# A conformer layer on one NeuronCore: x1 in one VectorE instruction from PSUM, three buffers behind silu, the layer norm and the gate in another order, three ada units ahead of x

## The chip, the cores and the metric

The kernel runs on one core of a Trainium2 chip. Its time is device time in microseconds (us); below, the median of three runs. The engines are PE (TensorE matmul; PEld is its weight load), DVE (VectorE), ACT (ScalarE), POOL (GpSimd) and SP (SyncE, which here only issues DMAs). Each engine has its own instruction stream, written by hand, and engines meet only at semaphores, so an instruction that waits holds up all that stands behind it on its engine.

## What is computed

One decoder layer (`DEPTH = 1`, so only mixer kind 0) on 512 tokens with 2048 features: adaLN modulation, RMS norm, conformer convolution, gated residual, RMS norm, squared-ReLU MLP, gated residual, RMS norm.

```python
def rms_norm(x, g):
    return x * lax.rsqrt(jnp.mean(x * x, axis=-1, keepdims=True) + EPS) * g

def conformer_conv(h, w_in, b_in, w_dw, b_dw, ln_g, ln_b, w_out, b_out):
    u = h @ w_in + b_in
    a, gt = jnp.split(u, 2, axis=-1)
    u = a * jax.nn.sigmoid(gt)
    u = causal_depthwise_conv_31(u, w_dw) + b_dw
    u = jax.nn.silu(layer_norm(u, ln_g, ln_b))
    return u @ w_out + b_out

cs = jax.nn.silu(c)
sh1, sc1, g1, sh2, sc2, g2 = split(cs @ ada_w + ada_b, 6)
h = rms_norm(x, norm1_g) * (1 + sc1) + sh1
x = x + g1 * conformer_conv(h, ...)
h = rms_norm(x, norm2_g) * (1 + sc2) + sh2
x = x + g2 * (jnp.square(jax.nn.relu(h @ w1)) @ w2)
return rms_norm(x, final_g)
```

(The three functions are shortened; `causal_depthwise_conv_31` stands for the library call.)

## The kernel before

**Layout.** Activations lie with features on the 128 partitions: 16 chunks of 128 features by 512 tokens. All is float32. A product of fp32 precision is made of three matmuls: each operand is split in a high part (`whi`, `hhi`, `dhi`, rounded to fp32r by ACT) and a low part (`wlo`, `hlo`, `dlo`, the remainder, by DVE or POOL), and PE adds hi*hi, hi*lo and lo*hi.

**Units.** Weights come in units of 128 x 2048 (1 MB). SP loads them into the four slots of `raw`, ACT makes `whi` (L625, `split_hi`), DVE (L942, `split_lo`) or POOL (L1255) makes `wlo`, and PE runs 48 matmuls of 512 columns on them. There are only two slots of `whi` and `wlo`, so the split of a unit waits for the unit two before it. The stages in order of time, named by their first unit:

- **A0**, 8 units: the first half of w_in, "outer": all eight PSUM banks collect at once while the chunks of h come one by one.
- **A1**, 24 units: the other columns of w_in, one bank each ("inner", `inner_unit`). For a feature chunk c the even bank holds the value half and the odd bank the gate half; ACT makes the sigmoid, DVE the product (`glu`, L986), and DVE, ACT and POOL share the 31 taps of the convolution: ACT begins two PSUM sums (`BEGIN`) and makes products (`SIDE`) that POOL adds up (L1283), DVE does the rest (L1002, `conv`). For chunk 15, the last, PE does ten taps with diagonal weights (L518), and DVE fourteen.
- **The layer norm** needs sums over features: PE multiplies by a column of ones (`token_sums`, L462; 128x1 outputs), DVE makes mean and 1/variance (L1034 to L1041), ACT the square root (L634), PE spreads the four columns over all partitions (`spread`, L476, into a PSUM bank), and ACT copies mean and 1/std from PSUM to SBUF (`mu`, `rstd`, L638 and L640).
- **B0**, 8 outer units: the first half of w_out. For each chunk `z(k)` has DVE subtract the mean (L1050), multiply by `rstd` (L1058) and make `hlo` (L931), and ACT make silu (L773) and `hhi` (L777). silu has two buffers, so the silu of chunk k waits for `hlo` of k-2.
- **B1**, 8 inner units: the second half of w_out. x1 = x + g1*(y + b_out): ACT reads a bank and makes g1*y + g1*b_out into `sig` (`gated`, L791), DVE adds x (L1091), ACT squares into `sq` (L798), DVE adds up the squares (L951, one `sq` buffer).
- **C0** and on: the MLP, 8 outer units, then alternating units of w2 and w1, and at the end the last norm, in which DVE makes 11 chunks (L1248) and POOL 5 (L1298), and SP stores them (L386).

**Modulation.** The product with `ada_w` is not done on PE. `ada_reduce(a)` (L925, DVE) multiplies one 128 x 2048 unit by silu(c) and sums it; there are 96 such units, 1 MB each, loaded into four homes (two in `adar`, two slots of `raw`). The tables `ADA_LN`, `ADA_B0`, `ADA_B1`, `ADA_C0` say how many of them DVE does in the layer norm and behind each unit of B0, B1 and C0. Units 0 to 31 (sh1 and sc1) are done in A0, units 32 to 47 hold g1, 48 to 63 sc2, 64 to 79 sh2. Before, `gate1` (L1065, L1068) makes g1 and g1*b_out when all 48 are done.

**keep_busy** (L470) is a run of matmuls of 512 columns whose result nobody reads.

The order on every engine is as the code is written; SP's loads stand in one queue.

## Time and profile before

| | |
|---|---|
| median of 3 runs | 2037.58 us (2036.48 to 2037.75) |
| the profiled execution | 2036.65 us, of it span 2034.8 us |
| PE busy | 1979.2 us (97%) |
| DVE busy | 1074.0 us (53%) |
| ACT busy | 678.8 us (33%) |
| POOL busy | 258.6 us (13%) |
| DMA | 300.73 MB, mean 148 GB/s |
| PE waits for ACT sig L654 / DVE hlo L931 / ACT sig L791 | 11.8 / 8.4 / 4.9 us |
| PE waits for ACT hhi L645 / DVE quad L951 / ACT st L634 | 4.0 / 3.6 / 3.5 us |

The span runs from the first to the last instruction; 1.85 us lie around it in the profiled execution. PE is busy nearly throughout, but busy also counts fillers (`keep_busy`), one-column matmuls and matmuls at the lower of PE's two clock levels, which take twice as long. So the places to look at are those where a stage begins: the start, the layer norm, the step from B0 to B1, that from B1 to C0, and the end. From 640 to 2015 us PE does its matmuls with no gap.

### The profile page before, as it was taken

The numbers are of one execution on the slowest core, as the hardware profiler recorded it, in microseconds if no ns is written. First come the engines' busy times: TensorE is split into PE (matmuls) and PEld (weight loads), VectorE is DVE, ScalarE is ACT, GpSimd is POOL, SyncE is SP. The second block draws the span as 40 slices with busy tenths as digits, with TensorE's granted clock in tenths as the row PEclk, the third lists the DMA queues.
The fourth block names the chain that finished last, engine by engine and source line by source line (L and its number), as shares of the span: only waits on it lengthen the run. The fifth ranks groups of instructions, "written<-read, shape, count | busy, mean of one in ns | idle before, by whom it ended". The sixth has DMA issues, their size and how long they took to land.

```text
span 2034.8 us, 21613 instructions
## 1 busy us (share of the span) xinstructions
PE 1979.2 (97%) x8658; PEld 1619.2 (80%) x8658; DVE 1074.0 (53%) x1159; ACT 678.8 (33%) x747; POOL 258.6 (13%) x145
## 2 busy tenths in 40 slices
PE   6899999999999999999999999999999999999996
PEld 3678888778787888888888888888888888888885
DVE  5989999868897876233223223323322322333244
ACT  5454645543433322321331232123123213212333
POOL 0019999810000000000000000000000000000001
PEclk9999999989999999999999999999999999999998
DMA  9962222247796566222222222222222222222212
GB/s 396 378 268 101 103 88 99 103 166 288 301 402 230 222 247 251 103 104 85 101 100 88 100 103 89 97 103 91 94 103 84 102 103 85 100 103 85 100 62 83
DMA packets 46084, 300.73 MB, mean 148 GB/s; under 512 B 4704, under 2 KB 4704, under 8 KB 10976
## 3 DMA queue, kind: packets, MB, share of 16 engines
q1 hardware_dynamic: 46048, 300.29, 39.6%
q8 instruction: 18, 0.29, 0.1%
q14 instruction: 18, 0.15, 0.0%
HBM read 296.08 MB, written 4.19 MB: 148 GB/s over the span
## 4 chain that ended last, share of the span: by engine, by line
PE 88%; DVE 8%; DMA 1%; ACT 1%; issue 0%; SPq 0%; DVEq 0%; ACTq 0%
PE ps L395 58%; PE ps L400 29%; DVE raw L925 2%; DVE adar L925 2%; DVE wlo L942 1%; DMA adar<-ada 1%; DVE hlo L931 1%; PE ps L484 1%; DVE quad L938 0%; DMA xb<-xT 0%; DVE ps L1002 0%; DVE xb L1248 0%; ACT hhi L777 0%; PE ps L476 0%; ACT whi L625 0%
## 5 line engine op out<-in xcount | busy, mean ns | idle before, releaser
L395 PE MATMUL ps<-hhi,whi 128*128 128x512 f32 (+1 forms) x1792 | 652.1, 391 | 11.8 <-ACT sig L791 4.9
L395 PE MATMUL ps<-hlo,whi 128*128 128x512 f32 (+1 forms) x1792 | 651.8, 390 | 7.3 <-DVE hlo L931 7.3
L625 ACT ACTIVATE whi<-raw 128x2048 fp32r<-128x2048 f32 x176 | 336.3, 1911 | 616.1 <-PE ps L400 615.1
L400 PE MATMUL ps<-hhi,wlo 128*128 128x512 f32 (+1 forms) x1792 | 435.1, 389 | 0.0
L942 DVE TENSOR_TENSOR wlo<-raw,whi 128x2048 fp32r<-128x2048 f32 x151 | 346.0, 2291 | 121.5 <-ACT whi L625 121.5
L395 PEld LDWEIGHTS ps<-hhi,whi 128*128 128x128 f32 x1792 | 336.9, 189 | 87.2 <-issue 9.5
L395 PEld LDWEIGHTS ps<-hlo,whi 128*128 128x128 f32 x1792 | 336.9, 188 | 79.6 <-issue 6.2
L395 PE MATMUL ps<-dhi,whi 128*128 128x512 f32 x1024 | 397.0, 389 | 0.0
L395 PE MATMUL ps<-dlo,whi 128*128 128x512 f32 x1024 | 397.0, 389 | 0.0
L400 PEld LDWEIGHTS ps<-hhi,wlo 128*128 128x128 f32 x1792 | 336.4, 188 | 69.9
L1181 DVE SCALAR_TENSOR_TENSOR xb<-ps,modb,xb 128x512 f32<-128x512 f32 x128 | 90.3, 746 | 363.2 <-PE ps L400 353.6
L400 PE MATMUL ps<-dhi,wlo 128*128 128x512 f32 x1024 | 253.9, 389 | 0.0
L1177 DVE TENSOR_TENSOR dlo<-quad,dhi 128x512 fp32r<-128x512 f32 x56 | 38.8, 693 | 392.3 <-ACT dhi L850 392.3
L1002 DVE SCALAR_TENSOR_TENSOR ps<-xb,pr,ps 128x502 f32<-128x502 f32 (+22 forms) x359 | 231.4, 728 | 3.2 <-ACT ps L702 3.2
L395 PEld LDWEIGHTS ps<-dhi,whi 128*128 128x128 f32 x1024 | 192.3, 188 | 40.0
L400 PEld LDWEIGHTS ps<-dhi,wlo 128*128 128x128 f32 x1024 | 192.2, 188 | 39.9
L395 PEld LDWEIGHTS ps<-dlo,whi 128*128 128x128 f32 x1024 | 192.1, 188 | 39.9
L1298 POOL TENSOR_TENSOR xb<-xb,rstd 128x512 f32<-128x512 f32 x5 | 6.2, 1272 | 1606.8 <-ACT rstd L640 1606.8
L844 ACT ACTIVATE quad<-ps 128x512 f32<-128x512 f32 x56 | 33.5, 598 | 412.8 <-PE ps L400 412.8
L1255 POOL TENSOR_TENSOR wlo<-raw,whi 128x2048 fp32r<-128x2048 f32 x25 | 115.8, 4631 | 147.7 <-ACT whi L625 147.7
L925 DVE SCALAR_TENSOR_TENSOR adar<-adar,csb 128x2048 f32<-128x2048 f32 x40 | 90.8, 2283 | 16.0 <-DMA adar<-ada 15.9
L925 DVE SCALAR_TENSOR_TENSOR raw<-raw,csb 128x2048 f32<-128x2048 f32 x42 | 96.0, 2298 | 3.7 <-DMA raw<-ada 3.7
(122 smaller groups left out, 772.6 us busy)
## 6 DMA issues: line engine op xcount, KB each, us to landing
raw<-w SPq DMA_DIRECT2D x176, 1024.0 KB, 4.8
raw<-ada SPq DMA_DIRECT2D x56, 1024.0 KB, 7.0
adar<-ada SPq DMA_DIRECT2D x40, 1024.0 KB, 7.3
xb<-xT SPq DMA_DIRECT2D x8, 1024.0 KB, 8.7
out<-xb SPq DMA_DIRECT2D x5, 512.0 KB, 4.2
out<-xb SPq DMA_DIRECT2D x6, 256.0 KB, 3.7
csb<-c SPq DMA_DIRECT2D x1, 1024.0 KB, 4.7
quad<-c SPq DMA_DIRECT2D x1, 1024.0 KB, 6.8
```

Source lines behind the costliest of these rows:

```text
L395: return pe.matmul(ps[:, bank, :], whi[:, slot, tile * P:(tile + 1) * P], x, start=first, stop=False, skip_group_check=True)
L400: return pe.matmul(ps[:, bank, :], wlo[:, slot, tile * P:(tile + 1) * P], x, start=False, stop=last, skip_group_check=True)
L484: last = pe.matmul(ps[0:1, 6, :], ones[:], x_squares[k % 2][:], start=k == 0, stop=k == KC - 1, skip_group_check=True)
L625: act.activation(whi[:, q % WS, :], raw_slot(q), ACT.Copy).then_inc(whi_done, 1)
L844: act.activation(relus[j % 2][:], ps[:, bank, :], ACT.Relu).then_inc(relu_done, 1)
L925: dve.scalar_tensor_tensor(s, s, 1.0, cs[:], ALU.mult, ALU.mult, accum_out=mod[:, a:a + 1]).then_inc(ada_used, 1)
L931: dve.tensor_tensor(ch(hlo, k), src[:], f(ch(hhi, k)), ALU.subtract).then_inc(hlo_done, 1)
L942: dve.tensor_tensor(wlo[:, q % WS, :], raw_slot(q), f(whi[:, q % WS, :]), ALU.subtract).then_inc(wlo_done, 1)
L1002: dve.scalar_tensor_tensor(out, ch(xb, c, 0, T - back), col("w_dw", c * TAPS + j), out, ALU.mult, ALU.add).then_inc(dv, 1)
L1177: dve.tensor_tensor(ch(dlo, j % BLK), squares[j % 2][:], f(ch(dhi, j % BLK)), ALU.subtract).then_inc(dlo_done, 1)
L1181: dve.scalar_tensor_tensor(ch(xb, n), ps[:, 4 + n % 4, :], modb[:, M_G2 + n:M_G2 + n + 1], ch(xb, n), ALU.mult, ALU.add).then_inc(x2_done, 1)
L1255: pool.tensor_tensor(wlo[:, q % WS, :], raw[:, q % RAW, :], f(whi[:, q % WS, :]), ALU.subtract).then_inc(wlo_done, 1)
```

## The change

- **Start.** SP loads ada units 0, 1 and 2 ahead of x, and ada unit 3 ahead of the first weight unit. ACT squares x into four buffers; DVE adds two squares each, and PE sums eight pairs in place of 16 squares.
- **1/std.** ACT takes the root straight from the sums in PSUM (scale 1/D, bias eps) and DVE the reciprocal; before, DVE did scale and reciprocal, ACT the root. In the first norm DVE's reciprocal stands behind ACT's root, which stands behind `split_hi(0)`. In the later norms DVE reads 1/std of the first chunk from PSUM and copies it to `rstd` itself.
- **Chunk 15.** Its gate half comes before its value half (the two last units of A1 change places), so that its sigmoid is made during the last unit. DVE has 13 taps for it, POOL five additions in place of four.
- **Layer norm.** Of three ada units one is left, and it stands ahead of the last glu. The 16 fillers ahead of B0 go.
- **B0.** silu has three buffers (`sig` is the third).
- **B1.** g1 is made in two halves. ACT adds g1*b_out to x beforehand (`bias_x`), and DVE makes x1 with one instruction that reads the bank. The first eight x1 follow one another. Squares have two buffers.
- **B1 to C0.** PE sums the last square straight from `sig`; fillers (2, 2 and 4) stand between its steps in place of 8 ahead of C0. DVE's split of unit C0+1 comes behind the first chunks of h2. Of the ada units 1, 14, 20 and 15 are done in the layer norm, B0, B1 and C0; before, 3, 14, 19 and 14.
- **End.** 3 and 4 fillers; DVE's last products wait for the spread alone, and PE spreads a second time for ACT's copy, which POOL uses.

```diff
-SIDE_LAST = 5
+SIDE_LAST = 6
...
-ADA_LN = 3
-ADA_B0, ADA_B1, ADA_C0 = (0, 0, 1, 1, 3, 3, 3, 3), (0, 2, 3, 3, 3, 3, 3, 2), (2, 2, 2, 2, 2, 2, 1, 1)
+ADA_LN = 1
+ADA_B0, ADA_B1, ADA_C0 = (0, 0, 1, 1, 3, 3, 3, 3), (1, 2, 3, 3, 3, 3, 3, 2), (3, 2, 2, 2, 2, 2, 1, 1)
...
-        x_squares = (sig, pacc)
-        scaled, normed, silus = (ta, s1), (tb, s2), (sq, pacc)
+        x_squares = (sig, pacc, tb, sq)
+        scaled, normed, silus = (ta, s1), (tb, s2), (sq, pacc, sig)
         normed2 = (ta, s1, tb, s2)
+        x1_squares = (sq, sig)
...
             load_ada0(0)
-            load_x(0)
-            load_x(1)
             load_ada0(1)
-            load_x(2)
-            load_x(3)
+            load_ada0(2)
+            for i in range(4):
+                load_x(i)
             sp.dma_start(pr[:], par).then_inc(par_in, 16)
-            load_ada0(2)
+            load_ada0(3)
             load_unit0(0)
-            load_ada0(3)
...
-            pe.wait_ge(s2_done, LATE + 1)
             pe.wait_ge(glu_done, KC)
-            token_sums(2, 0, s2, True)
...
-            keep_busy(16, 6, B0 + 1)
+            pe.wait_ge(rstd_done, 3)
             outer_units(B0, KC)
...
             for s in range(2):
-                pe.wait_ge(yg_done, s + 1)
+                pe.wait_ge(x1_done, s + 1)
                 inner_unit(s, s, B1 + s)
...
-            pe.wait_ge(ss1_done, KC)
-            token_sums(2, 0, ssum, True).then_inc(stat_done, 1)
+            pe.wait_ge(ss1_done, KC - 1)
+            token_sums(2, 0, ssum, True)
+            keep_busy(2, 5, C0)
+            pe.wait_ge(x1sq_done, KC)
+            token_sums(2, 0, sig, False).then_inc(stat_done, 1)
+            keep_busy(2, 5, C0)
             pe.wait_ge(root_done, 3)
             spread(3, 8)
-            keep_busy(8, 5, C0 + 1)
+            keep_busy(4, 5, C0 + 1)
...
+            def root(n, bank):
+                act.wait_ge(stat_done, n)
+                if n == 1:
+                    act.wait_ge(eps_set, 1)
+                act.activation(st[:, 4:8], ps[:, bank, 0:4], ACT.Sqrt, scale=1.0 / D, bias=eps[:]).then_inc(var_done, 1)
...
             split_hi(0)
-            root(1, 7)
+            root(1, 5)
+            copy_rstd(1, 7)
...
+            def bias_x(n):
+
+                act.wait_ge(xr_in[n // 4], 16)
+                act.activation(ch(xb, n), ch(xb, n), ACT.Identity, bias=g1b[:, n:n + 1]).then_inc(x1_biased, 1)
...
+            act.wait_ge(small, SMALL_G1 - 2)
+            for n in range(8):
+                bias_x(n)
+            split_hi(B1 + 1)
+            for n in range(8):
+                x1_square(n)
             act.wait_ge(small, SMALL_G1)
...
+            for n in range(8, KC):
+                bias_x(n)
+            for j in range(7):
+                split_hi(B1 + 2 + j)
+                x1_square(8 + j)
...
+            def inverse(n):
+                dve.wait_ge(var_done, n)
+                dve.reciprocal(st[:, 8:12], st[:, 4:8]).then_inc(root_done, 1)
...
-            ada_reduce(2)
-            dve.wait_ge(stat_done, 1)
-            variance(5)
+            inverse(1)
             ada_reduce(3)
             split_lo(0)
...
-                dve.wait_ge(yg_done, n + 1)
-                dve.wait_ge(xr_in[n // 4], 16)
-                dve.tensor_tensor(ch(xb, n), sig[:], ch(xb, n), ALU.add).then_inc(x1_done, 1)
+                if n < 7:
+                    dve.wait_ge(bank_done, 7 + n + 1)
+                else:
+                    dve.wait_ge(unit_done, B1 + n - 7)
+                dve.wait_ge(x1_biased, n + 1)
+                dve.scalar_tensor_tensor(ch(xb, n), ps[:, n if n < 8 else n % 2, :], modb[:, M_G1 + n:M_G1 + n + 1],
+                                         ch(xb, n), ALU.mult, ALU.add).then_inc(x1_done, 1)
```

How the order of instructions moves is shown at three places. The first is DVE from the last tap of chunk 15 to the first chunk of B0; `raw` and `adar` rows of 128x2048 are ada units. Before:

```order
484 L1002 SCALAR_TENSOR_TENSOR ps<-xb,pr,ps 128x492
485 L1009 TENSOR_TENSOR quad<-ps,quad 128x512
486 L1015 TENSOR_TENSOR xb<-ps,quad 128x512
487 L1016 TENSOR_TENSOR xb<-xb,ps 128x491
488 L925 SCALAR_TENSOR_TENSOR raw,mod<-raw,csb 128x2048
489 L1034 TENSOR_SCALAR st<-ps 128x4
490 L925 SCALAR_TENSOR_TENSOR raw,mod<-raw,csb 128x2048
491 L1037 TENSOR_TENSOR st<-st 128x4
492 L1039 SCALAR_TENSOR_TENSOR st<-ps,st 128x4
493 L1040 TENSOR_SCALAR st<-st 128x4
494 L1041 RECIPROCAL st<-st 128x4
495 L925 SCALAR_TENSOR_TENSOR adar,mod<-adar,csb 128x2048
```

The same place in the changed kernel (line numbers are its own):

```order
493 L1022 SCALAR_TENSOR_TENSOR ps<-xb,pr,ps 128x492
494 L1029 TENSOR_TENSOR quad<-ps,quad 128x512
495 L1035 TENSOR_TENSOR xb<-ps,quad 128x512
496 L1036 TENSOR_TENSOR xb<-xb,ps 128x491
497 L1059 TENSOR_SCALAR st<-ps 128x4
498 L1061 TENSOR_TENSOR st<-st 128x4
499 L1063 SCALAR_TENSOR_TENSOR st<-ps,st 128x4
500 L1064 TENSOR_SCALAR st<-st 128x4
501 L1065 RECIPROCAL st<-st 128x4
502 L1073 TENSOR_TENSOR quad<-xb,quad 128x512
503 L1085 TENSOR_TENSOR quad<-quad,ps 128x512
504 L1088 COPY rstd<-ps 128x512
```

Three ada units have left this stretch, and a copy of 1/std has come in behind the first chunk.

The second place is DVE from the last unit split of B0 to the first x1 (L1091, and L1124 in the changed kernel). Before:

```order
558 L942 TENSOR_TENSOR wlo<-raw,whi 128x2048
559 L925 SCALAR_TENSOR_TENSOR adar,mod<-adar,csb 128x2048 x2
560 L1065 TENSOR_TENSOR modb<-mod,pr 128x16
561 L1068 TENSOR_TENSOR g1b<-modb,pr 128x16
562 L925 SCALAR_TENSOR_TENSOR raw,mod<-raw,csb 128x2048
563 L1091 TENSOR_TENSOR xb<-sig,xb 128x512 x3
```

And now:

```order
560 L943 SCALAR_TENSOR_TENSOR adar,mod<-adar,csb 128x2048 x2
561 L1096 TENSOR_TENSOR modb<-mod,pr 128x8
562 L1098 TENSOR_TENSOR g1b<-modb,pr 128x8
563 L943 SCALAR_TENSOR_TENSOR raw,mod<-raw,csb 128x2048
564 L960 TENSOR_TENSOR wlo<-raw,whi 128x2048
565 L943 SCALAR_TENSOR_TENSOR raw,mod<-raw,csb 128x2048
566 L943 SCALAR_TENSOR_TENSOR adar,mod<-adar,csb 128x2048 x2
567 L960 TENSOR_TENSOR wlo<-raw,whi 128x2048
568 L943 SCALAR_TENSOR_TENSOR raw,mod<-raw,csb 128x2048 x2
569 L943 SCALAR_TENSOR_TENSOR adar,mod<-adar,csb 128x2048
570 L1124 SCALAR_TENSOR_TENSOR xb<-ps,modb,xb 128x512 x8
```

The gate (two rows of 128x8) has moved ahead of two splits; three ada units still stand between the last split of B0 and the first x1.

The third place is SP's queue at the start. Before, and then now:

```order
1 L270 DMA csb<-c 128x2048
2 L264 DMA adar<-ada 128x2048
3 L267 DMA xb<-xT 128x4x512 x2
4 L264 DMA adar<-ada 128x2048
5 L267 DMA xb<-xT 128x4x512 x2
6 L277 DMA pr<-par 128x736
7 L264 DMA raw<-ada 128x2048
8 L258 DMA raw<-w 128x2048
9 L264 DMA raw<-ada 128x2048
```

```order
1 L279 DMA csb<-c 128x2048
2 L273 DMA adar<-ada 128x2048 x2
3 L273 DMA raw<-ada 128x2048
4 L276 DMA xb<-xT 128x4x512 x4
5 L285 DMA pr<-par 128x736
6 L273 DMA raw<-ada 128x2048
7 L267 DMA raw<-w 128x2048
```

The first weight unit (`raw<-w`) was the ninth transfer of 1 MB beside the small `pr`, and is now the tenth; the last quarter of x was the seventh and is the eighth.

## Rows read from the trace of the kernel before

**Rows 1.** Page, part 2: busy tenths, and GB/s, in 40 slices of 50.9 us.

```profile
PE   6899999999999999999999999999999999999996
...
DVE  5989999868897876233223223323322322333244
...
GB/s 396 378 268 101 103 88 99 103 166 288 301 402 230 222 247 251 103 104 85 101 100 88 100 103 89 97 103 91 94 103 84 102 103 85 100 103 85 100 62 83
```

**Rows 2.** Start of the kernel: the issues of two loads, and their time to landing.

```profile
L258 SPq DMA_DIRECT2D raw<-w x1: 2467/2467/2467, 12.1 to 12.1; - x1
L264 SPq DMA_DIRECT2D raw<-ada x1: 571/571/571, 14.6 to 14.6; - x1
...
DMA to landing us min/median/max: 14.9/14.9/14.9
```

**Rows 3.** Timeline of the start: start us, us, engine, line, what, idle before.

```profile
28.62 1.89 ACT L625 ACTIVATE whi<-raw 128x2048 fp32r<-128x2048 f32 x1
...
30.14 2.26 DVE L925 SCALAR_TENSOR_TENSOR raw<-raw,csb 128x2048 f32<-128x2048 f32 x1
30.42 0.19 ACT L634 ACTIVATE st<-st 128x4 f32<-128x4 f32 x1
...
34.53 0.68 DVE L938 TENSOR_TENSOR quad<-xb,rstd 128x512 f32<-128x512 f32 x1
```

**Rows 4.** Timeline around the layer norm, DVE.

```profile
401.15 0.75 DVE L986 SCALAR_TENSOR_TENSOR xb<-ps,pr,sig 128x512 f32<-128x512 f32 x1 [3.15 <-ACT sig L690]
...
411.81 0.69 DVE L1009 TENSOR_TENSOR quad<-ps,quad 128x512 f32<-128x512 f32 x1
...
413.84 2.95 DVE L925 SCALAR_TENSOR_TENSOR raw<-raw,csb 128x2048 f32<-128x2048 f32 x1
...
425.03 0.69 DVE L1058 TENSOR_TENSOR quad<-quad,rstd 128x512 f32<-128x512 f32 x1
```

**Rows 5.** The same stretch, POOL.

```profile
408.90 1.26 POOL L1283 TENSOR_TENSOR quad<-quad,adar 128x506 f32<-128x506 f32 x1
```

**Rows 6.** The same stretch, PE.

```profile
414.89 1.79 PE L462 MATMUL ps<-ones,sig 128*128 128x1 f32 x8
...
420.06 2.07 PE L476 MATMUL ps<-ident,st 128*128 128x128 f32 x8 [1.05 <-ACT st L634]
421.78 5.47 PE L470 MATMUL ps<-whi 128*128 128x512 f32 x16
428.56 1.63 PE L395 MATMUL ps<-hhi,whi 128*128 128x512 f32 x6 [1.30 <-ACT hhi L777]
```

**Rows 7.** Timeline of ACT in B0.

```profile
448.59 0.82 ACT L773 ACTIVATE pacc<-s,pr 128x512 f32<-128x512 f32 x1 [1.36 <-DVE s L1058]
...
451.29 0.82 ACT L773 ACTIVATE quad<-quad,pr 128x512 f32<-128x512 f32 x1 [1.36 <-DVE quad L1058]
...
505.80 1.92 ACT L625 ACTIVATE whi<-raw 128x2048 fp32r<-128x2048 f32 x1 [8.96 <-PE ps L400]
```

**Rows 8.** Timeline of PE where B1 starts.

```profile
521.53 0.80 PE L395 MATMUL ps<-hhi,whi 128*128 128x512 f32 x1 [4.94 <-ACT sig L791]
```

**Rows 9.** Windows of 2 us there: window, length, busy of five engines, granted clock.

```profile
522.00:524.00 2.00, 2.00 (x6) 1.54 (x6) 1.48 (x3) 0.43 (x1) 0.00 (x0) 0.50 1.03 434
526.00:528.00 2.00, 2.00 (x7) 1.60 (x6) 1.43 (x3) 1.70 (x3) 0.00 (x0) 0.60 1.03 434
```

**Rows 10.** Timeline of PE between B1 and C0.

```profile
615.36 1.05 PE L462 MATMUL ps<-ones,quad 128*128 128x1 f32 x8 [3.64 <-DVE quad L951]
...
622.48 2.33 PE L395 MATMUL ps<-hhi,whi 128*128 128x512 f32 x8
```

**Rows 11.** The same stretch, ACT.

```profile
611.76 0.78 ACT L791 ACTIVATE sig<-ps,g1b,modb 128x512 f32<-128x512 f32 x1 [3.13 <-PE ps L400]
```

**Rows 12.** Timeline of the end, DVE.

```profile
2021.42 6.66 DVE L1248 TENSOR_TENSOR xb<-xb,ps 128x512 f32<-128x512 f32 x11 [2.82 <-ACT rstd L640]
```

**Rows 13.** The same stretch, SP's store issues.

```profile
2022.73 9.11 SPq L386 DMA_DIRECT2D out<-xb  x11
```

More of the change, by code:

```diff
@@ L238, in wait_ada, with shifts_until @@
                 eng.wait_ge(g2_in[a % 2], 16 * ((a - G2_LATE) // 2 + 1))
+        def shifts_until(k):
+            return next(j + 1 for j in range(8) if k < SH2_EARLY + sum(ADA_C0[:j + 1]))
         def adds_until(c):
@@ L293, in _ @@
             sp.wait_ge(ada_used, ADA0)
-            with loop(ET.SP, 0, 6) as i:
+            with loop(ET.SP, 0, 5) as i:
                 for q in range(RAW):
                     load_unit(A1 + 2 + q, 4 * i)
+            for q, unit in ((B0 - 2, B0 - 1), (B0 - 1, B0 - 2), (B0, B0), (B0 + 1, B0 + 1)):
+                sp.wait_ge(wlo_done, q - RAW + 1)
+                sp.dma_start(raw[:, q % RAW:q % RAW + 1, :], w[:, unit:unit + 1, :]).then_inc(raw_in[q % RAW], 16)
             def x_again(g):
@@ L481, in _ @@
             pe.wait_ge(ones_set, 1)
-            for k in range(KC):
-                pe.wait_ge(xsq_done, k + 1)
-                last = pe.matmul(ps[0:1, 6, :], ones[:], x_squares[k % 2][:], start=k == 0, stop=k == KC - 1,
+            for i in range(KC // 2):
+                pe.wait_ge(pair_done, i + 1)
+                last = pe.matmul(ps[0:1, 6, :], ones[:], x_squares[2 * i % 4][:], start=i == 0, stop=i == KC // 2 - 1,
                                  skip_group_check=True)
@@ L764, in _ @@
             c_square(KC - 1)
-            root(2, 2, 0)
+            act.wait_ge(ln_var, 1)
+            act.activation(st[:, 8:12], st[:, 4:8], ACT.Sqrt).then_inc(root_done, 1)
+            act.wait_ge(spread_done, 2)
+            act.activation(mu[:], ps[:, 0, :], ACT.Copy).then_inc(rstd_done, 1)
+            preload(ACT.Silu)
             def z(k):
@@ L776, in z @@
                     act.wait_ge(ac, k)
-                    act.activation(ch(hhi, k - 1), silus[(k - 1) % 2][:], ACT.Copy).then_inc(hhi_done, 1)
-            for k in range(6):
+                    act.activation(ch(hhi, k - 1), silus[(k - 1) % 3][:], ACT.Copy).then_inc(hhi_done, 1)
+            for k in range(7):
                 z(k)
@@ L810, in _ @@
-            x1_square(6)
-            for j in range(8):
-                n = 8 + j
-                x1_square(n - 1)
-                if j == 7:
-                    preload(ACT.Sqrt)
-                act.wait_ge(unit_done, B1 + j + 1)
-                gated(n, j % 2)
-                if j < 7:
-                    split_hi(B1 + j + 2)
-            x1_square(15)
+                if n >= 2:
+                    act.wait_ge(ss1_done, n - 1)
+                act.activation(x1_squares[n % 2][:], ch(xb, n), ACT.Square).then_inc(x1sq_done, 1)
@@ L821, in _ @@
+            act.wait_ge(small, SMALL_G1 - 2)
[4 more added lines that the diff above has]
+                x1_square(n)
+            act.wait_ge(small, SMALL_G1)
+            for n in range(8, KC):
[3 more added lines that the diff above has]
+                x1_square(8 + j)
+            preload(ACT.Sqrt)
+            x1_square(KC - 1)
+            root(2, 2)
             split_hi(C0 + 1)
-            root(3, 3)
@@ L953, in _ @@
             dve.wait_ge(cs_ready, 1)
-            ada_reduce(0)
-            ada_reduce(1)
+            for a in range(3):
+                ada_reduce(a)
+            for i in range(KC // 2):
+                one, two = x_squares[2 * i % 4], x_squares[2 * i % 4 + 1]
+                dve.wait_ge(xsq_done, 2 * i + 2)
+                dve.tensor_tensor(one[:], one[:], two[:], ALU.add).then_inc(pair_done, 1)
             dve.wait_ge(par_in, 16)
@@ L1077, in _ @@
                     split_lo(B0 + 1 + j)
-                    for k in range(4 * j + 2, min(4 * j + 6, KC + 2)):
+                    for k in range(4 * j + 3, min(4 * j + 7, KC + 3)):
                         z(k)
```

181 lines of the change are left out of this document (91 added, 90 removed).

## The prediction, made before the changed kernel ran

> **What bounds the kernel now.** I read the slices of the page first [rows 1]: PE is busy in nine tenths or more from the third slice to the last but one, except that busy counts fillers and slow matmuls. DVE is as busy as PE in the first four slices and again up to the eighth. Then I read who waits for whom: PE's waits name few places, and all stand where a stage begins. So the cost of a change is what it does to the first useful matmul of A0, B0, B1 and C0, and to the end. Between these points PE's stream is fixed: 48 matmuls of 0.227 us, 10.88 us, for each unit, and the changed kernel has the same units. I therefore follow the timeline from one such point to the next.
>
> **Two levels of PE's clock.** Where PE's matmuls of 512 columns stop for some microseconds, the granted clock falls from full (2.4 GHz) to half (1.2 GHz), and rises again after a stretch of steady matmuls. Where B1 starts it is 0.50 in the window from 522 and rises in that from 526 [rows 9]: a full window holds some nine matmuls, these hold six and seven. From 521.53 [rows 8] to about 527.4 PE runs at half, so such a start loses half of 5.9, **2.9 us**. Ahead of B0 the fillers took this loss: 16 of them last 5.47 us in place of 3.6 [rows 6]. That is the price of each start at the lower level below.
>
> **Start: +1.7.** In A0 DVE is never idle [rows 1]: each pair of chunks takes four ada units, a split and small work. So A0 moves with the first product of x and 1/std, 34.53 [rows 3]. Ahead of it DVE does ada unit 3 from 30.14 and a split. In the changed kernel ada unit 3 stands behind the reciprocal, which needs ACT's root, which stands behind ACT's `split_hi(0)`. That split needs the first weight unit. It was issued at 12.08 and landed 14.9 later, at 27.0; ada unit 3, the next megabyte, was issued at 14.59 and landed at 29.5 [rows 2]. The two change places in the queue, so the weights land at 29.5. Split 1.9 (1.89 before [rows 3]), root 0.2, reciprocal 0.2, and four handoffs of 0.03: ada unit 3 starts at 31.85 in place of 30.14, **+1.7**. The squares gate nothing: the last quarter of x lands at about 23.7 (a megabyte takes 2.5), its fourth square is done at 26.0, the pair at 26.7, PE at 27.8, where it was 28.1. Bounds: +0.7, if the weights are there in time (ACT's split then ends at 30.5 [rows 3], and only the root and the reciprocal come on top), and +2.6, if the queue is a third of a megabyte slower. A1 follows A0 in full: PE has no gap in it, and DVE waits for PE at its end. The split that now stands behind the first glu costs DVE 0.5 at the head of A1, which the two microseconds that it waits for chunk 14's sigmoid take up.
>
> **Layer norm: -4.75** at the first matmul of B0. Times here are those of before; the shift of the start comes on top.
> - Chunk 15's glu started at 401.15, behind a sigmoid of 0.7 [rows 4]. Now the sigmoid is done, and it starts at 400.45.
> - DVE has 13 taps of 0.65 in place of 14, so its taps would end 1.35 sooner. POOL has a fifth addition: the fourth ended at 410.16 [rows 5], and 410.16 - 0.7 + 1.4 is 410.9. DVE's three last additions took from 411.81 to 413.9 [rows 4]: chunk 15 is done at 413.05, -0.85.
> - The mean no longer waits for an ada unit of 2.95 [rows 4], nor the variance for another. PE's sums of squares, 1.79 at the lower clock [rows 6], end at 415.8, four small operations of DVE at 416.5, the root at 416.7. PE's two spreads of 2.07 and some 1.75 [rows 6] end at 419.5.
> - The third ada unit is gone, and the first product reads PSUM: it starts at 419.6, where it was 425.03 [rows 4], -5.4.
> - From this product to the first matmul of B0 it took 3.5 us (to 428.56 [rows 6]). Now the copy of 1/std, 0.65 as any read of 512 columns from PSUM (the glu, of three operands, takes 0.75 [rows 4]), comes between, because ACT makes the second silu before the first `hhi`: 4.2 us. First matmul at 423.8.
> Bounds: -3.5 (PE's one-column work slower, the copy dearer) and -5.8.
>
> **B0 up to B1: -2.0.** Before, B1 started 93.0 after B0 (521.53 - 428.56), though B0's 384 matmuls take 87.0: PE waited 4.94 us for the gate [rows 8], 0.4 for a split that stood behind z in ACT's queue, and the rest is drain. z took 2.7 a chunk, which the two silu buffers set (448.59 to 451.29 [rows 7]); with three buffers DVE's three operations set it, 1.85. So the splits behind z come in time, and DVE is through with z 4 us sooner. The gate for chunks 0 to 7 is made 27 us before it is needed. What is late next? The first x1 stands behind three ada units on DVE. PE's last but one unit ends, ACT splits (505.80, 1.92, which starts 0.3 behind PE [rows 7]), DVE splits 2.2, does three ada units of 2.2 (30.14 for one [rows 3]) and the first x1, 0.7: 11.9 in all, against 10.9 of PE's last unit. PE waits 1.0. The start of B0 now is at the lower clock, since no filler stands there: +2.9. So 87.05 + 2.9 + 1.0 = 91.0, **-2.0**. Hidden on ACT: eight `bias_x` of 0.6 fit in its idle 9 us between two splits [rows 7].
>
> **B1's clock: -2.9.** A wait of 1.0 us is shorter than the 1.3 that stood ahead of B0, behind the fillers, with the clock at full in what followed [rows 6]; I take it that the clock stays. Inside B1 ACT has eight more `bias_x`, behind the second half of the gate, and then the split that the third unit needs: by the same counting it is ready at 20.3 after B1's start, needed at 21.8. Bound: 0, if the clock falls all the same.
>
> **B1 to C0: -5.2.** Before: gate 0.78 from 611.76 [rows 11], x1, the addition of square 14, square 15, its addition, then PE's sums at 615.36 [rows 10], variance, root, spread 2.07 at half clock, ACT's copy, h2, and C0 at 622.48 [rows 10] behind the fillers: 10.7 in all. Now: x1 0.75, square 0.65, sums 0.95, root 0.2, reciprocal 0.2, spread 1.0, h2 0.75, `hhi` 0.7, eight handoffs 0.3: 5.5. Its 0.35 of half clock at 622.48 (2.33 for eight, 1.98 elsewhere) goes too. One ada unit fewer stands on DVE in the layer norm and one more in B1, and the last addition of squares stands ahead of x1: by a count of 10.05 of DVE work a unit against 10.88 of PE, DVE is some 0.4 late with the last x1. -5.2 - 0.35 + 0.4 = **-5.2** when rounded. Bounds: -5.9 (DVE in time) and -1.8 (the clock falls, below). In C0 three ada units stand ahead of the fourth chunk's `hlo`; it is ready 2 us or more before PE needs it.
>
> **End: -0.4.** DVE's last products start when the spread is done, not after ACT's copy (2021.42 [rows 12]), some 1.4 sooner. But SP's eleven store issues follow one another without a gap for 9.11 us [rows 13], and the second waits for POOL, which still needs ACT's copy behind a second spread. Only SP's first issue gains in full; I take 0.4. Bounds: -1.3 and +1.3 (clock at half in both spreads).
>
> **Sum.** 1.7 - 4.75 - 2.0 - 2.9 - 5.2 - 0.4 = -13.55. The profiled execution took 2036.65, so 2023.1; the median of the runs is 0.93 above it: **2024.0**.
>
> **A rule against the change.** In the layer norm the clock fell at about 414.95, with PE's wide matmuls over since 411.3 and only one-column sums and pauses since (there the sums slow from 0.95 to 1.79 [rows 6]). The gap ahead of C0 is now 5.5 us with eight fillers in it, 1.8 us of matmuls. The Trainium skill, "TensorE: Matmul & The Clock Gate", section "What's actually happening", says that the default state is throttled and that activity releases it; by that a thin filling may not hold the clock. No run here shows a gap filled like this one. Its time is rival B.
>
> **Rivals.**
> - **B, the clock falls** in the filled gap ahead of C0 (or in the 1.0 ahead of B1). For: at half clock began B1 [rows 9], and C0's first eight matmuls [rows 10]. Against: the fillers. Price: half of six microseconds, 2.9, and in C0 a spread at half clock, 1.05, less what passes before the fall: 3.5. Time 2027.5.
> - **C, the step to B1 doesn't shrink.** The gate comes early, but DVE's x1 stands behind as many ada units as before, and if DMA makes it wait, as it did for some 2.4 us in all, or z saves less, PE still waits 4 us, the clock falls: 3.0 + 2.9, and the x1 come late for C0 also, 1.0. Time 2030.9. For: DVE was busy without a break there. Against: the same waits now fall into DVE's slack behind the splits.
> - **D, slower.** B1 has 20 ada units in place of 19 and DMA moves 402 GB/s in its slice [rows 1]; 4.19 MB for each unit of 10.88 us are 385. If its loads came late, PE would wait in each of seven units. The point: it must lose 17.7 us (13.6 and 4.1) for a loss over 0.2%, 2.5 a unit, a rate of 313 GB/s. Time 2042. Against: DVE had no wait for DMA in B1 before, and the bytes are the same.
>
> **Chances.** Forecast 0.63, B 0.15, C 0.12, D 0.03, 0.03 for a case between C and D, and 0.04 for more gain than forecast, about 2020.5 (start at +0.7, layer norm at -5.8, C0 at -5.9). The range from 2020.5 to 2029.5 holds the forecast with its bounds and B and leaves out C and D and part of the last. Within 0.2% (4.1 us, about what a measurement can tell from no change) lies only the case between C and D. Faster 0.94, slower 0.03.
>
> **What would show it.** DVE's first product of A0 at 36.2; B0's first matmul at about 425.5 (423.8 + 1.7) with a granted clock of 0.50; one wait of PE of about 1 us where B1 starts, at about 516.5, clock at 1.00; C0's first matmul 5.5 to 6 us behind B1's last, at full clock; SP's issues at the end still without a gap. I am wrong if the clock is 0.50 behind either gap, if DVE's first x1 comes over 2 us behind PE's last matmul of B0, or if `split_hi(0)` doesn't wait for its weights.

## The result, and the profile after

The changed kernel takes **2025.68 us** (median of 5, 2025.49 to 2026.14) against 2037.58 before: 0.9944 of it, 95% interval 0.9932 to 0.9956. Forecast were 2024.0 and a range of 2020.5 to 2029.5. The profiled execution is one of 2026.14 with a span of 2024.4, 10.5 less than the profiled one before; the other 1.4 of the medians' 11.9 is the scatter of these two executions, and the working below goes by the profiled ones.

The same slices as in [rows 1], page of the changed kernel, busy tenths:

```profile
PE   5989999989999999999999999999999999999997
...
DVE  5989999969898875233323323322322322333244
```

They show that the bound is what it was. What differs is read where a stage begins. First the start (start, length, engine, line, what, idle before), which answers to [rows 3]:

```profile
18.00 1.87 PE L494 MATMUL ps<-sig,ones 128*1 128x512 f32 x2 [18.00 <-DVE sig L977]
...
26.90 0.63 ACT L672 ACTIVATE sig<-xb 128x512 f32<-128x512 f32 x1 [0.86 <-PE ps L494]
...
30.93 0.59 ACT L674 ACTIVATE quad<-ps 1x512 f32<-1x512 f32 x1 [1.84 <-PE ps L494]
31.42 1.89 ACT L643 ACTIVATE whi<-raw 128x2048 fp32r<-128x2048 f32 x1
33.22 0.24 ACT L654 ACTIVATE st<-ps,eps 128x4 f32<-128x4 f32 x1
33.59 2.26 DVE L943 SCALAR_TENSOR_TENSOR raw<-raw,csb 128x2048 f32<-128x2048 f32 x1
...
37.98 0.69 DVE L956 TENSOR_TENSOR quad<-xb,rstd 128x512 f32<-128x512 f32 x1
```

The copy of the row of sums (30.93) waits for PE, and the first product of x comes at 37.98, 3.45 later than before. ACT's split follows the row copy at once: it does not wait for its weights, which is one of the signs of being wrong that the prediction had named.

The layer norm, DVE and PE, which answers to [rows 4] to [rows 6]:

```profile
414.70 0.69 DVE L1029 TENSOR_TENSOR quad<-ps,quad 128x512 f32<-128x512 f32 x1 [0.53 <-POOL quad L1320]
416.87 1.87 PE L472 MATMUL ps<-ones,xb 128*128 128x1 f32 x8 [0.88 <-DVE xb L1036]
418.60 1.84 PE L472 MATMUL ps<-ones,sig 128*128 128x1 f32 x8
420.31 3.39 PE L486 MATMUL ps<-ident,st 128*128 128x128 f32 x16
423.81 0.69 DVE L1085 TENSOR_TENSOR quad<-quad,ps 128x512 f32<-128x512 f32 x1
427.94 3.75 PE L405 MATMUL ps<-hhi,whi 128*128 128x512 f32 x8 [4.23 <-ACT hhi L802]
```

DVE's last additions wait for POOL (0.53). Both kinds of one-column sums run at half clock, then PE stands idle for 4.23, and eight matmuls of B0 take 3.75 (1.98 at full clock). The granted clock, the last number but two in a row of windows, went up at the end of the spreads (0.71 in the window from 422, after 0.50) and fell again in the idle time:

```profile
424.00:426.00 2.00, 0.00 (x0) 0.00 (x0) 1.97 (x4) 1.31 (x3) 0.00 (x0) 1.00 1.02 426
426.00:428.00 2.00, 0.07 (x1) 0.10 (x1) 1.97 (x4) 1.54 (x3) 0.00 (x0) 0.65 1.02 430
428.00:430.00 2.00, 2.00 (x5) 1.61 (x6) 2.00 (x4) 1.53 (x3) 0.00 (x0) 0.50 1.01 426
```

B0 and the start of B1, which answer to [rows 7] to [rows 9]: the next z starts 1.81 after the one shown, with a wait of 0.47 (2.7 and 1.36 before), PE waits 0.81 and not 4.94, and B1's matmuls follow one another at full clock.

```profile
449.63 0.81 ACT L798 ACTIVATE sig<-quad,pr 128x512 f32<-128x512 f32 x1 [0.47 <-DVE quad L1085]
...
518.62 0.50 PE L405 MATMUL ps<-hhi,whi 128*128 128x512 f32 x1 [0.81 <-DVE xb L1124]
518.96 0.40 PE L405 MATMUL ps<-hlo,whi 128*128 128x512 f32 x1
```

B1 to C0, which answers to [rows 10]: PE's stream of B1 ends at 605.99 (3.79 from 602.20 on), the last x1 starts 0.73 behind it, and C0 begins at full clock, 6.83 behind the stream's end where the prediction looked for 5.5 to 6:

```profile
602.20 3.79 PE L410 MATMUL ps<-hhi,wlo 128*128 128x512 f32 x16
606.72 0.75 DVE L1124 SCALAR_TENSOR_TENSOR xb<-ps,modb,xb 128x512 f32<-128x512 f32 x1
...
609.91 1.16 PE L486 MATMUL ps<-ident,st 128*128 128x128 f32 x8
...
612.82 2.09 PE L405 MATMUL ps<-hhi,whi 128*128 128x512 f32 x8 [0.83 <-ACT hhi L844]
```

The end, SP's store issues as in [rows 13]: still without a gap.

```profile
2011.65 9.36 SPq L396 DMA_DIRECT2D out<-xb  x11
```

### The profile page after: what moved, and what is told of

Its sections match the earlier page's. It is cut to its first block, busy times and chain, and to the rows that moved or that the text cites. A ratio compares the mean times of both kernels' runs of the same rounds, so it can differ in the third digit from the quotient of the medians.

```text
span 2024.4 us, 21590 instructions
## 1 busy us (share of the span) xinstructions
PE 1969.6 (97%) x8649; PEld 1616.0 (80%) x8649; DVE 1078.6 (53%) x1167; ACT 675.9 (33%) x746; POOL 261.6 (13%) x146
## 4 chain that ended last, share of the span: by engine, by line
PE 86%; DVE 9%; POOL 1%; issue 1%; ACT 1%; DMA 1%; SPq 0%; POOLq 0%; DVEq 0%; ACTq 0%
PE ps L405 57%; PE ps L410 28%; DVE raw L943 2%; DVE adar L943 2%; DVE wlo L960 2%; DMA xb<-xT 1%; DVE hlo L949 0%; DVE quad L956 0%; ACT xb L815 0%; DVE quad L969 0%; POOL wlo L1292 0%; DVE xb L1124 0%; PE ps L472 0%; PE ps L494 0%; POOL quad L1320 0%
## 5 line engine op out<-in xcount | busy, mean ns | idle before, releaser
L1022 DVE SCALAR_TENSOR_TENSOR ps<-xb,pr,ps 128x504 f32<-128x504 f32 (+22 forms) x358 | 230.7, 729 | 3.2 <-ACT ps L721 3.2
```

The source lines that it names most:

```text
L1022: dve.scalar_tensor_tensor(out, ch(xb, c, 0, T - back), col("w_dw", c * TAPS + j), out, ALU.mult, ALU.add).then_inc(dv, 1)
```

## The experiments

All are the changed kernel with the edit shown. Each is timed beside the kernel before; the ratios have intervals of about 0.0015 to either side, so that gains of a microsecond or two are read from the rows, and the times only tell that they arrive. The kernel before took 2036.9 beside e1 to e8 and 2037.4 beside e9 to e12, up to 0.7 less than beside the changed kernel, so a difference to its 2025.68 is uncertain by as much. Lines are those of each kernel.

### The start: what holds the row of sums?

**e1, PE warmed up.**

```diff
             pe.wait_ge(ones_set, 1)
+            pe.wait_ge(cs_ready, 1)
+            for _ in range(8):
+                pe.matmul(ps[:, 0, :], csb[:, 0:P], csb[:, 0:T], start=True, stop=True, skip_group_check=True)
             for i in range(KC // 2):
```

> The changed kernel, with eight fp32 matmuls of 512 columns on the loaded constants ahead of the sums of squares at the start of the kernel (they write a bank of PSUM that the first real sum overwrites). In the changed kernel PE's first wide sums stand at 18.00 and take 1.87 for two, later 1.02; they free DVE's ring of squares late, the row copy comes at 30.93 (28.13 before) and the first product of x and 1/std at 37.98. Theory W (the slow first sums hold up the ring): with PE already at full clock when they come, two sums take 1.0 from the first, the row copy comes at 28.0 to 29.0, the first product at 35.5 to 36.3, the kernel 2023.5 to 2024.3, 0.9932 to 0.9937 of before. Rival (the order of loads and DVE's own work set the row copy): row copy at 30.9, product at 38.0, 2025.7, 0.9944.

Measured 2023.85 (0.9935). Timeline:

```profile
18.28 1.02 PE L497 MATMUL ps<-sig,ones 128*1 128x512 f32 x2 [1.40 <-DVE sig L980]
21.33 1.02 PE L497 MATMUL ps<-sig,ones 128*1 128x512 f32 x2 [0.99 <-DVE sig L980]
...
25.49 0.63 ACT L675 ACTIVATE sig<-xb 128x512 f32<-128x512 f32 x1 [0.85 <-PE ps L497]
...
29.52 0.59 ACT L677 ACTIVATE quad<-ps 1x512 f32<-1x512 f32 x1 [1.83 <-PE ps L497]
```

The sums take 1.02 from the first, the row copy is 1.41 earlier and the first product too (36.57). That is less than theory W expected (row copy at 28.0 to 29.0), although the time lies in its range. Every four squares still take 3.05, though PE works 2.04 in them, and ACT still waits 0.85 for a buffer: something beside PE's speed holds them.

**e2, loads and ada units in the old order.**

```diff
             load_ada0(0)
+            load_x(0)
+            load_x(1)
             load_ada0(1)
-            load_ada0(2)
-            for i in range(4):
-                load_x(i)
+            load_x(2)
+            load_x(3)
             sp.dma_start(pr[:], par).then_inc(par_in, 16)
-            load_ada0(3)
+            load_ada0(2)
             load_unit0(0)
+            load_ada0(3)
...
-            for a in range(3):
-                ada_reduce(a)
+            ada_reduce(0)
             for i in range(KC // 2):
+                if i == 4:
+                    ada_reduce(1)
...
+            ada_reduce(2)
             inverse(1)
```

> The changed kernel with the order of loads and of ada units at the start put back as it was before (one ada unit ahead of x, one after four pairs, the third behind the squares; the first weight unit ahead of ada unit 3), while the squares stay in pairs and the second half of the start (1/std ahead of ada unit 3) stays. If the order of loads is what cost the start 3.45, the row copy is back at 28.1 and the first product of x is at 34.5 or sooner: about 2022.5, 0.9929 of before. If it is the pairs (one sum of PE for two squares, DVE waiting for PE's slow first sums), the row copy stays at 30 or later and the time within 0.5 of 2025.7.

Measured 2023.24 (0.9931). The row copy is at 28.56 and the first product at 35.61. So with the pairs kept, the order of the loads is worth 2.37 of the 3.45: x is there sooner, and what the squares wait for is hidden again. The product is not back at 34.5. Of the 1.1 that stay, 0.4 are in the row copy (28.56 for 28.13); the rest lies behind it, where the root now stands behind the split, which was not tried apart in this order.

**e5, six buffers for the squares.**

```diff
-        x_squares = (sig, pacc, tb, sq)
+        x_squares = (sig, pacc, tb, sq, ssum, ta)
...
-                if k >= 4:
-                    act.wait_ge(xsq_used, k // 2 - 1)
-                act.activation(x_squares[k % 4][:], ch(xb, k), ACT.Square).then_inc(xsq_done, 1)
+                if k >= 6:
+                    act.wait_ge(xsq_used, k // 2 - 2)
+                act.activation(x_squares[k % 6][:], ch(xb, k), ACT.Square).then_inc(xsq_done, 1)
```

(and `% 6` where DVE and PE take them)

> The changed kernel with six buffers for the squares of x at the start in place of four (two more that are idle there). With PE warmed up the sums took 1.02 each from the first, and the row copy still came only 1.4 sooner (29.52 for 30.93): four squares took 3.04, in which PE's two sums take 2.04, and ACT waited 0.85 for a buffer of the ring. Theory R (the ring of four is the bound: square, sum of a pair on DVE, PE's sum and four handoffs in a circle): with six, ACT's squares run ahead up to what has landed, and the row copy comes at 28.5 to 29.7 with PE's slow first sums (four sums of 1.7, four of 1.02 from 18.0, no gap: 28.9), the first product at 35.6 to 36.8: 1.2 to 2.4 less than 2025.7, 0.9932 to 0.9938. Rival (x itself lands too late): row copy at 30.5 or later, no change.

Measured 2024.64 (0.9941). Timeline:

```profile
28.27 0.59 ACT L674 ACTIVATE quad<-ps 1x512 f32<-1x512 f32 x1 [1.84 <-PE ps L494]
29.83 1.91 ACT L643 ACTIVATE whi<-raw 128x2048 fp32r<-128x2048 f32 x1 [0.97 <-DMA raw<-w]
31.64 0.25 ACT L654 ACTIVATE st<-ps,eps 128x4 f32<-128x4 f32 x1
...
36.41 0.68 DVE L956 TENSOR_TENSOR quad<-xb,rstd 128x512 f32<-128x512 f32 x1
```

The row copy is 2.66 earlier, though PE's sums are still slow at first. Theory R holds. Only now does the split wait for its weights, which land at 29.8, and the first product comes at 36.41. This is the chain that the prediction had worked out, with 29.5, 31.85 and 36.2.

**e10, six buffers and the root ahead of the split**, with **e9** as the changed kernel again on the same chip.

```diff
-            split_hi(0)
             root(1, 5)
+            split_hi(0)
```

> The changed kernel again, unedited, on the chip and beside the kernel before that the next three are timed with, so that gains of one to two microseconds can be read. Both theories: 2025.0 to 2026.2, 0.9944 of before.

> The changed kernel with six buffers for the squares and the root ahead of split_hi(0) on ACT. With six buffers alone the row copy came at 28.27 and the first weight unit became what is waited for: the split started when it landed, 29.83, the root stood behind it (31.64), ada unit 3 began at 32.02 and the first product at 36.41. Theory: with the root first, the root is at 29.1, ada unit 3 starts at 29.4, runs beside the split (29.83 to 31.7), and the first product comes at 34.0 to 34.2: 2.3 less than with six buffers alone, 3.9 less than the changed kernel, 2021.8, 0.9925 of before. Rival (the loads of A0 are then what is late, at 400 GB/s and more): DVE waits for DMA in A0 and the gain at the head of A1 is 2 or less of the 3.9.

Measured: e9 2025.67 (0.9942); e10 2022.42 (0.9928), 3.25 less. Timeline of e10:

```profile
29.77 0.26 ACT L654 ACTIVATE st<-ps,eps 128x4 f32<-128x4 f32 x1 [1.14 <-PE ps L499]
34.55 0.68 DVE L956 TENSOR_TENSOR quad<-xb,rstd 128x512 f32<-128x512 f32 x1
```

I had left out PE's eight one-column matmuls behind the row copy (1.14), so the root is at 29.77 and not 29.1. The first product is back where it was before the change (34.53), and all of it arrives: A1's sums start at 400.26, where they were at 400.23 before and at 403.69 in the changed kernel, and DVE waits for no load in A0. So, with the new order of the loads, the 3.45 are the ring of four (1.57, e5) and the root behind the split (1.86, e10 against e5). This and the 2.37 of e2 are two ways of undoing the same loss and don't add: the ring costs time here because the first square starts at 15.97, where it is 11.52 in e2.

### The pause ahead of B0

**e3, sixteen fillers put back.**

```diff
+            keep_busy(16, 6, B0 + 1)
             pe.wait_ge(rstd_done, 3)
             outer_units(B0, KC)
```

> The changed kernel with the sixteen filling matmuls put back between the layer norm's spreads and the first matmul of B0. In the changed kernel PE waits 4.23 there, the clock is 1.00 in the window 424 to 426 and 0.50 in 428 to 432. Theory F (the pause lets the clock fall, and the spreads had raised it): sixteen fillers at full clock take 3.6, end before hhi comes at 427.9, and the first eight matmuls of B0 take 1.98 in place of 3.75, B0 at full clock: 2.5 to 2.9 less, about 2023.0, 0.9931 of before. Rival G (the clock at 424 to 426 does not last, as before where sixteen took 5.47): fillers end about 1.2 late, B0 then is at full clock: 2.9 - 1.2, 1.7 less, 2024.0, 0.9936. Rival H: fillers late and the clock at half in B0 all the same: +1.2, 2026.9, 0.9950.

Measured 2024.42 (0.9938). PE:

```profile
423.55 3.89 PE L480 MATMUL ps<-whi 128*128 128x512 f32 x16
428.03 2.09 PE L405 MATMUL ps<-hhi,whi 128*128 128x512 f32 x8 [0.59 <-ACT hhi L803]
...
607.46 2.00 PE L486 MATMUL ps<-ident,st 128*128 128x128 f32 x8
```

Theory F holds at its place: the fillers run at full clock, B0 too, and from B0's first matmul to B1's it is 88.14 in place of 90.68, 2.54 less. The time shows 1.3 of it. 0.84 went in another place: from B1's first matmul to C0's it is 95.04 in place of 94.20. In this execution the clock fell in the filled gap there (the spread takes 2.00, with the changed kernel 1.16).

The 2.54 hang on the profile that they are taken from. The same unedited kernel in e9:

```profile
427.58 3.58 PE L405 MATMUL ps<-hhi,whi 128*128 128x512 f32 x8 [4.23 <-ACT hhi L802]
...
608.53 2.08 PE L486 MATMUL ps<-ident,st 128*128 128x128 f32 x8
```

There B0's first matmul to B1's takes 89.67, since half clock ends sooner, and against that the fillers gain 1.53. The clock fell in the filled gap too (95.11 from B1's first matmul to C0's), so that against e9 nothing is lost there. The fillers are thus worth 1.5 to 2.5 at their place. In e9, as in e1, e4, e6, e7 and e10, the sixteen spread matmuls took 3.76, at half clock to their end, and 3.37 to 3.59 in the other profiles. Rival G would be fillers behind such slow spreads; no profile shows that. In the three profiles with fillers (e3, e11, e12) they ran at full clock.

### The waits at B1

**e4, one ada unit more ahead of the first x1.**

```diff
-ADA_B0, ADA_B1, ADA_C0 = (0, 0, 1, 1, 3, 3, 3, 3), (1, 2, 3, 3, 3, 3, 3, 2), (3, 2, 2, 2, 2, 2, 1, 1)
+ADA_B0, ADA_B1, ADA_C0 = (0, 0, 1, 1, 2, 3, 3, 4), (1, 2, 3, 3, 3, 3, 3, 2), (3, 2, 2, 2, 2, 2, 1, 1)
```

> The changed kernel with one ada unit more ahead of the first x1 of B1: the eighth unit of B0 has four in place of three, the fifth two in place of three. PE's wait at the head of B1, 0.81, becomes 0.8 + 2.2 = 3.0. Theory S (after a wait of about a microsecond the clock stays, after 4.94 it fell): at 3.0 it falls or it does not; if it falls, B1 starts at 0.50 and the kernel loses 2.2 + 2.9 = 5.1, less what one late x1 gives back: 2030.5, 0.9968. If it stays at 3.0, the loss is 2.2: 2027.9, 0.9955. If another engine than DVE sets the first x1, the wait grows by less than 1 and the time stays within 1 of 2025.7.

Measured 2028.69 (0.9961). PE:

```profile
519.51 0.64 PE L405 MATMUL ps<-hhi,whi 128*128 128x512 f32 x1 [3.02 <-DVE xb L1124]
...
523.26 0.39 PE L405 MATMUL ps<-hlo,whi 128*128 128x512 f32 x1
```

The wait is 3.02 as expected: DVE sets the first x1. Eight matmuls follow at half clock, 0.43 apart in place of 0.23, 1.6 in all and not 2.9. Half clock ends 3.4 after the pause, where it lasted 5.9 before [rows 9]. In the changed kernel 0.81 cost none. That the shorter pause made the penalty shorter isn't shown: ahead of B0 one and the same pause was followed by very different stretches of half clock (last section).

**e6, ada units dealt out otherwise.**

```diff
-ADA_B0, ADA_B1, ADA_C0 = (0, 0, 1, 1, 3, 3, 3, 3), (1, 2, 3, 3, 3, 3, 3, 2), (3, 2, 2, 2, 2, 2, 1, 1)
+ADA_B0, ADA_B1, ADA_C0 = (0, 0, 2, 1, 3, 3, 3, 2), (3, 2, 3, 3, 3, 3, 3, 0), (3, 2, 2, 2, 2, 2, 1, 1)
```

> The changed kernel with the ada units of the last units of B0 and of B1 dealt out otherwise: the last unit of B0 has two in place of three ahead of the first x1, the last of B1 none in place of two, the others take them up. PE's wait of 0.81 at the head of B1 should go, and the last x1 of B1, 0.87 behind PE in the changed kernel, should be on time: 1.7 less, about 2024.0, 0.9936 of before. Rival (the last x1 is late because of the handoffs from PE over ACT, not because DVE is behind): only 0.8 less, 2024.9. Rival 2 (DVE, with three units in each of the middle units, falls behind there and PE waits inside B1): no gain or a loss.

Measured 2022.94 (0.9934). DVE and PE:

```profile
604.61 0.75 DVE L1124 SCALAR_TENSOR_TENSOR xb<-ps,modb,xb 128x512 f32<-128x512 f32 x1 [4.73 <-PE ps L410]
...
610.68 2.09 PE L405 MATMUL ps<-hhi,whi 128*128 128x512 f32 x8 [0.81 <-ACT hhi L844]
```

PE has no wait where B1 starts, DVE now waits for PE with the last x1, and from B0's first matmul to C0's it is 182.61 in place of 184.88, 2.27 less. From that x1 to C0 it still takes 6.07 (6.10 in the changed kernel): this part is a chain of handoffs, and no ada unit stands in it.

**e8, two silu buffers.**

```diff
-        scaled, normed, silus = (ta, s1), (tb, s2), (sq, pacc, sig)
+        scaled, normed, silus = (ta, s1), (tb, s2), (sq, pacc)
...
-                    if k >= 3:
-                        act.wait_ge(hlo_done, KC + k - 2)
+                    if k >= 2:
+                        act.wait_ge(hlo_done, KC + k - 1)
```

(and `lo_part(k - 2, ...)` in place of `k - 3` on DVE)

> The changed kernel with two silu buffers in B0 in place of three. In the changed kernel DVE waits 1.55 and 1.95 for ACT behind the last two splits of B0, so it has some slack. Theory (the third buffer is what brought z down from 2.7 to about 1.9 a chunk, and with that the wait at B1): z takes 2.7 again, PE waits about 0.4 for a split behind z and, since DVE's slack of 3.5 behind the splits is less than the 13 or so that z grows by on 16 chunks, 1 to 4 more at the head of B1 and the clock falls there: 2027 to 2031. Rival (DVE has slack enough since the gate is made sooner; the third buffer gives nothing): within 0.5 of 2025.7, 0.9944.

Measured 2030.38 (0.9969), 4.7 more. What DVE waits for from B0's start to B1's, e8:

```profile
DVE hlo L949 <- ACT hhi L802: 9.4, 11, 1.4
DVE wlo L960 <- ACT whi L643: 8.1, 3, 3.9
DVE adar L943 <- DMA adar<-ada: 2.3, 4, 1.2
DVE raw L943 <- DMA raw<-ada: 0.6, 1, 0.6
```

and the changed kernel:

```profile
DVE wlo L960 <- ACT whi L643: 16.6, 6, 8.7
DVE hlo L949 <- ACT hhi L802: 0.8, 1, 0.8
```

With two buffers DVE waits 8.6 more for silu and 8.5 less for splits: its slack pays for it. But it then meets the loads, whose slots it frees later, and waits 2.9 for them. PE waits 4.79 for x1 (as before for the gate), B1 starts at half clock for some 5.7, and B0's first matmul to B1's is 95.46 in place of 90.68. That is rival C, priced at 2030.9, come true in a kernel with one buffer less. So the gate made early would, it seems, have gained little at B1 by itself; a kernel with that alone was not run.

### The filled gap ahead of C0

**e7, without the fillers there.**

```diff
-            keep_busy(2, 5, C0)
             pe.wait_ge(x1sq_done, KC)
             token_sums(2, 0, sig, False).then_inc(stat_done, 1)
-            keep_busy(2, 5, C0)
...
-            keep_busy(4, 5, C0 + 1)
+            pe.wait_ge(whi_done, C0 + 1)
```

> The changed kernel without the eight filling matmuls between the last sums of B1 and C0. In the changed kernel the clock is 1.00 from B1 into C0. Theory of the prediction's rival B turned round (the thin filling holds the clock): without it the gap of 7.0 is idle but for one-column sums, the clock falls, the spread takes 2.1 in place of 1.2 and C0 begins with 2.1 for eight matmuls at 3.6 to 4.1: 3 to 4 more, about 2029.0, 0.9961 of before. Rival (a gap this short does not cost the clock whatever stands in it): no change, or a little less, since PE's own sums no longer stand behind fillers: 2025.4, 0.9943.

Measured 2027.44 (0.9957), 1.8 more. PE:

```profile
612.38 3.75 PE L405 MATMUL ps<-hhi,whi 128*128 128x512 f32 x8 [1.75 <-ACT hhi L842]
615.92 2.22 PE L405 MATMUL ps<-hlo,whi 128*128 128x512 f32 x8
```

The clock falls, and C0's first sixteen matmuls take 1.9 more; from B1's first matmul to C0's it takes 94.60, 0.4 more. So the fillers are worth about 2 and not 3 to 4. They don't hold the clock every time either. By the spread behind them (1.16 at full clock, 1.87 to 2.08 when it fell) it stayed at full in the profiles of the changed kernel, e1, e2, e5, e6, e8, e11 and e12, and fell within the gap in e3, e4, e9 and e10. One of these, e9, is the changed kernel itself. In e3, e9 and e10 that cost only 0.8 to 0.9, since the clock was back when C0 began. Against such an execution the fillers are worth about 1.4.

### All together

**e11** is e5, e10, e3 and e6 in one; **e12** is e11 with the loads and ada units of e2.

> The four edits together: six buffers for the squares, the root first, the sixteen fillers ahead of B0, and the ada units of B0 and B1 dealt out otherwise. If they add up: 3.9 at the start, 1.7 in B0's clock, 1.7 at B1 and C0, 7.3 less than the changed kernel: 2018.4, 0.9909 of before. Rival: the fillers, held at half clock in some executions as they were in the kernel before, come late, and only 5 to 6 are left: 2020.2.

> The same four edits, and the loads and ada units at the start in the order of the kernel before. The first product then comes at 33.2 to 34.0, as the third ada unit is done ahead of the reciprocal and x lands sooner: within 0.5 of the one above, 2018.0 to 2018.6. If the rows show a first product later than 34.2, the new order of the loads is the better one once the ring has six buffers.

Measured: e11 **2017.48** (0.9906, interval 0.9890 to 0.9921), 8.2 less than e9 on the same chip; e12 2018.63 (0.9908). The gains add up (7.3 were expected), and what is over them shows in e11's rows:

```profile
413.57 1.05 PE L472 MATMUL ps<-ones,xb 128*128 128x1 f32 x8 [0.87 <-DVE xb L1037]
414.48 1.25 PE L472 MATMUL ps<-ones,sig 128*128 128x1 f32 x8
...
423.27 2.08 PE L405 MATMUL ps<-hhi,whi 128*128 128x512 f32 x8 [0.58 <-ACT hhi L803]
```

In this execution the clock fell late, and both sums of the layer norm took 2.30. In e12 they took 1.87 and 1.84 and B0 starts 1.3 later, which is as much as the times differ. When the clock falls varies for one and the same kernel too (last section). So the order of the loads decides next to nothing once there are six buffers: in e12 ada unit 3 lands late (DVE waits 2.04 for it), and the first product is at 34.16, not in the 33.2 to 34.0 that were expected, against 34.69 in e11.

## Why the prediction was right, and where its steps were off

- **Start, +1.7 forecast, +3.45 measured.** The step that failed is "The squares gate nothing". I had ACT's four squares run as soon as x lands. They can't: a square's buffer comes free only after the second square, DVE's addition and PE's sum, and this circle lets four squares through in 3.05. The rest of the step (weights at 29.5, root behind the split, 36.2) was measured in e5 as 29.8 and 36.41. It is the size of the term that was wrong, and the bound of +2.6 too, and the sign for it came true: `split_hi(0)` didn't wait for its weights.
- **Layer norm, -4.75 forecast, -4.1 measured** (394.03 from A0's first product to B0's first matmul before, 389.96 after). POOL binding the last additions was forecast. What I left out are PE's eight sums of the chunk itself: they stand ahead of the sums of squares, also at half clock, 0.9 more. The end of it, 4.2 from product to matmul, measured 4.13. In the experiments that leave all of this stretch as it is (e4, e6, e7, e8 and e9), the 389.96 are 388.63 to 390.31, by the moment at which the clock falls; the 0.65 that I missed by is within that scatter.
- **B0 to B1, -2.0 forecast, -2.3 measured** (-3.3 by e9's profile, as half clock ended sooner there). The wait is 0.81 for 1.0, on DVE's x1 as forecast. e8 shows why it is so short: the third buffer.
- **B1's clock, -2.9 forecast, -2.8 measured** (PE's stream of B1 took 90.19 from 521.53 on, and takes 87.37 from 518.62 on). It stayed, as assumed, in every profile with a wait of 0.81.
- **B1 to C0, -5.2 forecast, about -4.2 measured** (from the end of B1's stream to C0's first matmul 10.76 before and 6.83 after, and 0.23 behind C0's start, where I had 0.35). From x1 to C0 eight steps took 6.1 where I had 5.5: each is 0.03 to 0.2 longer than the bare operation, 0.9 in all and not 0.3, the root 0.36 and not 0.2, the spread 1.2 and not 1.0. And x1 was 0.7 late, not 0.4: ACT does its eight `bias_x` in a row ahead of a split, and DVE stands idle for 5.28 behind it:

```profile
533.13 5.02 ACT L815 ACTIVATE xb<-xb,g1b 128x512 f32<-128x512 f32 x8 [2.72 <-DVE g1b L1098]
...
539.99 2.29 DVE L960 TENSOR_TENSOR wlo<-raw,whi 128x2048 fp32r<-128x2048 f32 x1 [5.28 <-ACT whi L643]
```

  That split was in time for PE, as counted; what the wait does to DVE's queue I had not counted. From there to the last x1 DVE has no other wait, so it can't catch up. In e6, where this wait is 1.81 and no ada unit stands ahead of the last x1, DVE is there 4.73 early.
- **End, -0.4 forecast, -0.5 measured** (19.33 from the end of PE's last unit, where its next sums start, to the end before, 18.82 after).
- **Rivals.** B didn't come in the profiled run, but it did in e9, the same kernel once more: the clock fell in the filled gap, and the time was 2025.67. So what was wrong in B is above all its price of 3.5. It cost 0.8 to 0.9 in e3, e9 and e10, where the clock was back at C0, and about 2 in e7 without any fillers. C is what happens with two silu buffers (e8). D has nothing in its favour: DVE waited for no load in B1.

The measured terms, 3.45 - 4.1 - 2.3 - 2.8 - 4.2 - 0.5, make -10.45, the difference of the profiled executions (10.4 by their spans); forecast was -13.55. The 3.1 between them are the start (1.75), the steps ahead of C0 (1.0), the sums in the layer norm (0.65) and B1's clock (0.1), less 0.4 gained elsewhere. The waits and the clock levels that the other terms named came as forecast. That the median is only 1.7 off is in part luck: the other 1.4 are the scatter of the profiled executions.

## What to carry to other kernels

A ring of buffers must be priced by its full circle, from first use to release with every handoff in it, and not by its slowest engine: here a third silu buffer was worth 4.7 us, and two more for the squares would have hidden nearly half of the new cost of the start. Work that is moved behind a long instruction on another engine waits for it even where each is small or hidden by itself (the root behind the split, 1.9). After a chain is shortened, place fillers anew: sixteen fillers that were late in the old gap fit the new one and gave back 1.5 to 2.5 at their place.
